# Expert passes of a mixture-of-experts kernel: the last chunk's matmuls in another order (transposes first, then both down products)

## The reference, cut to what matters

```python
def _swiglu(h, w_gate, w_up, w_down):
    return (jax.nn.silu(h @ w_gate) * (h @ w_up)) @ w_down

def _moe(h, w_router, w_gate, w_up, w_down):
    """Top-2-of-8 SwiGLU experts, softmax over the selected logits, sorted grouped dispatch."""
    ...
    hid = jax.nn.silu(lax.ragged_dot(xs, w_gate, group_sizes)) * lax.ragged_dot(xs, w_up, group_sizes)
    ys = lax.ragged_dot(hid, w_down, group_sizes)
    ys = ys * gates.reshape(-1)[order][:, None].astype(ys.dtype)
```

## Time and profile before

| | |
|---|---|
| three timed runs | 5582.97, 5589.52 and 5590.10 us, median 5589.52 |
| span of the profiled execution | 5587.1 us, given by its span alone |
| PE busy | 5157.5 us, 92% of the span |
| DVE, ACT, POOL busy | 49%, 40%, 6% of the span |
| expert passes | from 3370.5 us to the last down matmul at 5512.8 us |
| mean granted PE clock | 0.958 of full speed |

### The profile page before, as it was taken

One profiled execution on the slowest core, in us unless ns is written; L12 is line 12 of the kernel. 1 busy time (PEld: TensorE's weight loads), 2 busy tenths in 40 slices (PEclk: granted clock), 3 DMA queues, 4 the chain that ended last, 5 costly groups with the idle time before them and its releaser, 6 DMA issues. The chain is left out here.

```text
span 5587.1 us, 97211 instructions
## 1 busy us (share of the span) xinstructions
PE 5157.5 (92%) x38308; PEld 4523.6 (81%) x38309; DVE 2743.0 (49%) x4394; ACT 2225.6 (40%) x3437; POOL 342.1 (6%) x564
## 2 busy tenths in 40 slices
PE   7986989899899999997989988999999999999994
PEld 5675967677677899996867678989898999999994
DVE  2597545333834555554156434444444554555444
ACT  2454236333443444443234423333334444444432
POOL 0111100000600000000023001000000000000001
PEclk8997999999999999998999999999999999999997
DMA  2110010310003655553100425444444555555444
GB/s 88 35 66 17 0 37 1 134 51 30 8 12 123 244 209 205 191 208 115 46 16 19 139 113 185 155 157 158 164 158 175 184 195 186 194 196 188 181 157 188
DMA packets 104610, 688.52 MB, mean 123 GB/s; under 512 B 12320, under 2 KB 16304, under 8 KB 63280
## 3 DMA queue, kind: packets, MB, share of 16 engines
q1 hardware_dynamic: 90752, 639.74, 31.6%
q0 software_dynamic: 8816, 27.44, 1.3%
q10 hardware_dynamic: 4800, 17.83, 0.8%
HBM read 622.67 MB, written 62.29 MB: 123 GB/s over the span
## 5 line engine op out<-in xcount | busy, mean ns | idle before, releaser
L3374 DVE TENSOR_TENSOR experts_low<-experts_raw,experts_high 128x1024 fp32r<-128x1024 f32 x678 | 810.5, 1223 | 982.9 <-ACT experts_high L3301 982.9
L3236 PE MATMUL ps<-experts_xs_high,experts_high 128*128 128x256 f32 (+1 forms) x3584 | 1036.1, 289 | 39.0 <-issue 36.7
L3236 PE MATMUL ps<-experts_xs_low,experts_high 128*128 128x256 f32 (+1 forms) x3584 | 1034.3, 289 | 0.0
L3236 PE MATMUL ps<-experts_xs_high,experts_low 128*128 128x256 f32 (+1 forms) x3584 | 1034.3, 289 | 0.0
L3236 PEld LDWEIGHTS ps<-experts_xs_high,experts_high 128*128 128x128 f32 x3584 | 679.3, 190 | 50.5 <-issue 42.4
L3301 ACT ACTIVATE experts_high<-experts_raw 128x1024 fp32r<-128x1024 f32 x678 | 687.8, 1050 | 40.9 <-DMA experts_raw<-experts 40.9
L3236 PEld LDWEIGHTS ps<-experts_xs_low,experts_high 128*128 128x128 f32 x3584 | 679.4, 190 | 8.1
L3236 PEld LDWEIGHTS ps<-experts_xs_high,experts_low 128*128 128x128 f32 x3584 | 679.1, 189 | 0.4 <-issue 0.4
L2913 PE MATMUL ps<-dense_xs_parts,dense_high 128*128 128x256 f32 x2816 | 499.6, 280 | 7.0 <-DVE dense_low L3022 5.9
L2913 PEld LDWEIGHTS ps<-dense_xs_parts,dense_high 128*128 128x128 f32 x2816 | 437.0, 189 | 14.2 <-issue 7.8
L3228 PE MATMUL ps<-experts_high,experts_hid_high 128*128 128x512 f32 x1120 | 438.5, 392 | 0.0
(11 more groups left out here) (538 smaller groups left out, 9096.3 us busy)
## 6 DMA issues: line engine op xcount, KB each, us to landing
experts_raw<-experts SPq DMA_DIRECT2D x226, 1536.0 KB, 6.4
dense_raw<-dense SPq DMA_DIRECT2D x90, 1536.0 KB, 6.3
mixT<-w_in SPq DMA_DIRECT2D x36, 512.0 KB, 3.3
y_slot<-mla_blank SPq DMA_DIRECT2D x15, 1152.0 KB, 21.1
out_proj_raw<-w_out SPq DMA_DIRECT2D x48, 256.0 KB, 2.8
proj_keys_raw<-w_in SPq DMA_DIRECT2D x20, 512.0 KB, 3.2
x_mixed<-mixT SPq DMA_DIRECT2D x16, 512.0 KB, 2.6
h_rows<-out_proj_rows SPq DMA_DIRECT2D x16, 512.0 KB, 2.6
```

The source lines that it names most:

```text
L3236: last = nc.tensor.matmul(ps[:, m, 0:width], w[:, u, m, c], x[:, k, 0:width], start=(k == 0 and i == 0), stop=(k == KD - 1 and i == 2))
L3374: nc.vector.tensor_tensor(low[:, v, t, :], raw[:, v % NR, t, :], high[:, v, t, :].bitcast(F32), ALU.subtract).then_inc(split, 1)
```

## The change

In the last chunk of a pass the six turns stand together, directly behind the up product, each with the wait it had. After them come all tiles of down(v), and then down(u), with the waits for down(u)'s operands ahead of both. The number of matmuls and transposes is the same. The semaphore `down` gets its increment for down(v) later in the order. Nothing else is edited.

```diff
@@ -3260,33 +3260,26 @@
                     pe.wait_ge(split, 3 * n + SPLIT0)
                     core.settle(pe)
                     v = (u - 1) % NB
-                    if not (isinstance(f, int) and f == NC - 1):
+                    if isinstance(f, int) and f == NC - 1:
+                        for a in range(3):
+                            for h in range(2):
+                                if a:
+                                    pe.wait_ge(x_low, UNITS * (j + 1) + 2 * (a - 1) + h + 1)
+                                elif h == 0:
+                                    pe.wait_ge(gathered, 48 * (j + 2))
+                                    pe.wait_ge(hid_made, n + 2)
+                                core.settle(pe)
+                                turn(a, h)
+                        pe.wait_ge(hid_split, n + 1)
+                        pe.wait_ge(split, 3 * (n + 1) + SPLIT0)
+                        core.settle(pe)
+                    for a in range(n_tiles):
+                        last = down_tile(v, a, isinstance(f, int) and f == 1, False)
+                    last.then_inc(down, 1)
+                    if isinstance(f, int) and f == NC - 1:
                         for a in range(n_tiles):
-                            last = down_tile(v, a, isinstance(f, int) and f == 1, False)
+                            last = down_tile(u, a, False, True)
                         last.then_inc(down, 1)
-                        return
-                    for a in range(3):
-                        if a < n_tiles:
-                            last = down_tile(v, a, False, False)
-                            if a == n_tiles - 1:
-                                last.then_inc(down, 1)
-                        for h in range(2):
-                            if a:
-                                pe.wait_ge(x_low, UNITS * (j + 1) + 2 * (a - 1) + h + 1)
-                            elif h == 0:
-                                pe.wait_ge(gathered, 48 * (j + 2))
-                                pe.wait_ge(hid_made, n + 2)
-                            core.settle(pe)
-                            turn(a, h)
-                    pe.wait_ge(hid_split, n + 1)
-                    pe.wait_ge(split, 3 * (n + 1) + SPLIT0)
-                    core.settle(pe)
-                    for a in range(n_tiles):
-                        last = down_tile(u, a, False, True)
-                    last.then_inc(down, 1)
```

## The result

The changed kernel takes 5634.5 us (median, 5631.5 to 5640.3); the kernel before took 5587.9 beside it. The ratio is 1.0081, with a 95% interval of 1.0066 to 1.0095. I had forecast 5596, with a range up to 5612. It is slower by 47 us, twice what the first rival gave, so at least one thing besides that rival is at work.

A forecast was written before the change was run, and what follows sets the result against it. PE, busy 92%, was taken as the bound, so only its idle time and clock count. Borders +3.6 and clock +3 gave +6.6 on the 5587.1 us span; with the median 2.4 above the span, 5596, range 5585 to 5612.

The forecast's parts named there:

- the first rival: PE's instruction stream doesn't get past both down products, so border gaps keep their lengths: +24.4 us, 5614; chance 0.16.
- Part (a): Turns without down(v) ahead of them: down(u)'s old place is reached 0 to 0.3 us earlier, taken as 0.2.
- Part (b): Down(v) behind the turns: PE's last down matmul ends 3.5 us later in a wide pass, 2.6 in a narrow one.
- Part (c): Wait between the products, before down(u): its going away gains nothing, as no idle time stands there.
- (e): Borders: narrow to narrow -3.5, narrow to wide +2.6, last pass's end +3.5, behind wide passes +1; sum +3.6 us.
- (d): Border gaps hide the added matmuls: PE's stream leads by about 26 matmuls; its longer feed costs 0.3 to 0.5 us.
- Part (f): Clock falling in the tail, with PE partly idle among the turns: 1.6 us a fall, 0 to 8 us, taken as 3.
- The second rival: Clock falls in every tail and isn't hidden at wide borders either: +16.4 us, 5606; chance 0.10.

The follow-up runs named there:

- the held kernel: SP's 1.5 MB weight load at a pass's end held until the next pass's first gate product: changed kernel 5612.9 us, kernel before 5583.4 us.
- the filled pair: Changed kernel with narrow passes' three holes filled by extra matmuls, without and with the weight load held back: 5617.5 and 5608.0 us.

## Why the prediction was wrong, point by point

**Right.** Part (a): the turns came 0 to 0.25 us earlier, and the down products 0.2 (wide) and 0.1 (narrow) in a clean tail. Part (b): 3.4 and 2.6 us of added work against my 3.5 and 2.6. Part (c): nothing was gained from the wait between the products. In (e), ACT's silu is next in line once the border is short.

**The step that failed is (d), the cover.** I took the lead of PE's instruction stream as about 26 matmuls, from 155 against 129 between code loads, and so put the added matmuls into the gaps. The code loads show a load starting with 12.6 matmuls left, for 24 in line and, with the weight load held, for 32. Of the added work 1.2 us at a narrow border fit in; a wide tail of 16 stood near that lead already (2.4 to 2.9 us ahead). Behind wide passes PE resumed 3.9 to 7.2 us later than before, where I had put 0.3 each, and behind narrow ones 4.9 to 6.1, where I had put 0.1. The first rival, with its 24.4 us, described this, and I gave it 0.16. The count of the earlier trace rows went wrong because it took the time of a code load as a fixed place in the code. In the held kernel's first tail, with PE's rows as in the earlier trace rows, that load started 2.6 us behind the last up matmul, where it was 5.25 before. A single load dates nothing to within ten matmuls. I also read the windows of the earlier trace rows as landings; they show starts, and the load at 3661.1 to 3661.4 took 1.2 us more.

The Trainium skill, "TensorE: Matmul & The Clock Gate", in the section on the array's architecture, gives the queue 64 entries, which I had read as 32 matmuls with their weight loads. The runs don't bear that reading out: with 24 in line, and with 32 when the weight load was held, the code load started only some 12.6 matmuls, 25 instructions, ahead of the end.

**A second part of (d) was sized wrongly.** I noted that code might have to be loaded beside the weight load, but charged it at the wide borders alone, as 0 to 3 us in sum. By the filled pair it costs 1.2 us at each narrow border and 2.5 behind each wide pass, 11 us in sum: the load that comes late also comes into another's transfer, the second code load at a narrow border, the first already at a wide one. That is why the gaps grew where they should have shrunk.

**Part (f), the clock, was the right mechanism at a quarter of its size.** I took 3 us, with 8 as the bound. It measured 11.6 in the tails: it fell in six of eight, at 1.5 to 2.3 us each, since the turns themselves run slow too, not only the matmuls behind them. That it hides at wide borders held in the changed kernel, in the one case there: the second tail ends 1.6 us late, yet PE resumes at 23.2 against 22.9 behind the two clean ones. In the held kernel it didn't hide: 21.8 and 22.4 behind the slow tails, 20.2 behind the clean one. The filling of the narrow holes shows the cause; for the wide passes, where no bank was free, it was not tried. The second rival, the clock falling in every tail, was named with two sizes, 8 us in (f) and 12.8 in its own sum; the measured 11.6 lies between. The Trainium skill's "HAM oscillation" section of the same page tells of waits for DMA between groups of matmuls, behind each of which the clock is down again; here much shorter waits, holes of 0.7 to 1.4 us among transposes, brought it down in six of eight tails.

**The sum.** 23.9 moved + 11.6 clock in the tails + 7.9 gaps + 2.0 behind them = 45.4. The runs took away the collision (-21.6; in that execution two of the four narrow tails also ended at 12.5, at full clock, and the clock cost 8 us in the tails, not 11.6), the narrow holes (-17.0), and both (-26.5). What remains above before, 16 us, is less than the 23.9 of moved work, as the shorter gaps of the narrow borders and their full clock give some back.

**Left open:** why PE needs 5 to 8 us behind a wide pass even without the weight load, where a second code load comes 3 to 5 us behind the first. The jump over the narrow arm is a candidate; exchanging the arms was not tried. POOL's gather of rows moves data in that time too, and was not varied. What sets the lead of the stream was not varied by itself.

## What to carry to other kernels

Independent work between the links of a chain across engines isn't a detour to be tidied up: moved behind the chain it was paid nearly in full here (23.9 us), and the holes that it left cost half as much again through the clock (11.6). An idle gap put down to "issue" hides work only as far as the instruction stream runs ahead of the engine, which is to be measured by when the code load starts for tails of different lengths, and a code load that is put back can meet the next big transfer. What brought the next pass forward was an earlier release of the last wait before the border (1.5 to 1.7 us).

## What the runs showed of the hardware that was not expected

- With 16 matmuls of 512 columns in line, PE's next code load started 2.4 to 2.9 us before the last of them ended; with 24, or 32 and no weight load beside, 2.5 to 3.1, so a longer line puts it back by its own time.
- A 16 KB code load that follows its forerunner by 1.4 us at a narrow border with the weight load held follows it by 3.1 to 4.6 us beside that 1.5 MB load. With 32 in line the first code load itself started 0.1 to 0.7 us before the end instead of 2.9 to 3.1.
- Three holes of 0.7 to 1.4 us around pairs of transposes let the granted clock fall to 0.50 in six of eight tails (five of eight in the held kernel); one hole of up to 1.4 us did in none of eight.
- Six float32 matmul records (three instructions of the program), 2.74 us in all, kept the clock up over a narrow border without delaying the next pass.
